# SwiGLU's gate and up products computed channel by token, with 512- and 256-column matmuls, in a fused two-block kernel

## The reference

```python
h = rmsnorm(x, ffn_norm_w[l])
x = x + (jax.nn.silu(h @ w_gate[l]) * (h @ w_up[l])) @ w_down[l]
...
return rmsnorm(x, final_norm_w)
```

## Time and profile before

| what | value |
|---|---|
| median of three runs | 2379.36 us (2378.09 to 2380.82) |
| the profiled execution, its own time | 2380.18 us |
| its span, first to last instruction | 2378.4 us |
| TensorE matmul (PE) | 2362.0 us busy, 99%, 11452 instructions |
| TensorE weight load (PEld) | 1939.2 us, 82% |
| VectorE (DVE) | 1426.4 us, 60% |
| ScalarE (ACT) | 1183.9 us, 50% |
| GpSimd (POOL) | 241.7 us, 10% |

### The profile page before, as it was taken

One profiled execution on the slowest core, in us unless ns is written; L12 is line 12 of the kernel. 1 busy time (PEld: TensorE's weight loads), 2 busy tenths in 40 slices (PEclk: granted clock), 3 DMA queues, 4 the chain that ended last, 5 costly groups with the idle time before them and its releaser, 6 DMA issues.

```text
span 2378.4 us, 28485 instructions
## 1 busy us (share of the span) xinstructions
PE 2362.0 (99%) x11452; PEld 1939.2 (82%) x11452; DVE 1426.4 (60%) x1701; ACT 1183.9 (50%) x1695; POOL 241.7 (10%) x336
## 2 busy tenths in 40 slices
PE   9999999999999999999999999999999999999998
PEld 7887888888888888888887778788888888888887
DVE  6655665665566545665865565576554554557775
ACT  6544454454445444555655455465444444446554
POOL 0053004305300430000000010000000000000000
PEclk9999999999999999999999999999999999999999
DMA  6565457446545655666665454456555555655554
GB/s 211 195 173 164 142 178 190 157 154 183 167 137 182 174 169 169 222 206 194 211 216 190 142 179 149 152 179 227 186 188 195 189 184 194 193 181 193 195 194 142
DMA packets 241073, 430.79 MB, mean 181 GB/s; under 512 B 32212, under 2 KB 35933, under 8 KB 240942
## 3 DMA queue, kind: packets, MB, share of 16 engines
q1 hardware_dynamic: 227808, 413.38, 54.4%
q10 hardware_dynamic: 13134, 15.60, 2.2%
HBM read 423.66 MB, written 5.29 MB: 180 GB/s over the span
## 4 chain that ended last, share of the span: by engine, by line
PE 89%; POOL 5%; DVE 2%; DMA 1%; issue 1%; ACT 1%; ACTq 0%; SPq 0%; POOLq 0%; DVEq 0%
PE gemm L1328 27%; PE gemm L1330 27%; PE gemm L1329 27%; POOL arena L2283 5%; PE side L904 3%; DMA arena<-delta_blocks 1%; DVE arena L1751 1%; DVE weight_lo L1745 1%; PE side L1251 1%; PE side L998 0%; PE side L1266 0%; PE side L1290 0%; DMA arena<-in_x_dram 0%; PE side L1064 0%; PE side L1220 0%
## 5 line engine op out<-in xcount | busy, mean ns | idle before, releaser
L1745 DVE TENSOR_TENSOR weight_lo<-weight_raw,weight_hi 128x1024 fp32r<-128x1024 f32 x780 | 970.5, 1248 | 736.3 <-ACT weight_hi L1356 735.0
L1356 ACT ACTIVATE weight_hi<-weight_raw 128x1024 fp32r<-128x1024 f32 x780 | 821.9, 1056 | 863.2 <-PE gemm L1330 822.7
L1328 PE MATMUL gemm<-weight_hi,x_hi 128*128 128x512 f32 x2368 | 943.8, 399 | 1.1 <-DVE weight_lo L1745 1.1
L1330 PE MATMUL gemm<-weight_hi,x_lo 128*128 128x512 f32 x2368 | 924.6, 390 | 0.0
L1329 PE MATMUL gemm<-weight_lo,x_hi 128*128 128x512 f32 x2368 | 924.0, 390 | 0.0
L1328 PEld LDWEIGHTS gemm<-weight_hi,x_hi 128*128 128x128 f32 x2368 | 445.4, 188 | 100.2 <-issue 9.7
L1330 PEld LDWEIGHTS gemm<-weight_hi,x_lo 128*128 128x128 f32 x2368 | 445.2, 188 | 94.3
L1329 PEld LDWEIGHTS gemm<-weight_lo,x_hi 128*128 128x128 f32 x2368 | 445.9, 188 | 88.9 <-issue 1.4
L1328 PE MATMUL gemm<-weight_hi,lhs_hi 128*128 128x512 f32 x736 | 287.4, 390 | 0.0
L1330 PE MATMUL gemm<-weight_hi,lhs_lo 128*128 128x512 f32 x736 | 286.8, 390 | 0.0
L1329 PE MATMUL gemm<-weight_lo,lhs_hi 128*128 128x512 f32 x736 | 286.7, 390 | 0.0
(11 more groups left out here) (186 smaller groups left out, 1024.0 us busy)
## 6 DMA issues: line engine op xcount, KB each, us to landing
weight_raw<-in_w_in_dram SPq DMA_DIRECT2D x207, 1024.0 KB, 5.1
weight_raw<-in_w_out_dram SPq DMA_DIRECT2D x48, 1024.0 KB, 5.1
weight_raw<-in_w_gate_dram SPq DMA_DIRECT2D x44, 1024.0 KB, 5.2
weight_raw<-in_w_up_dram SPq DMA_DIRECT2D x44, 1024.0 KB, 5.1
weight_raw<-in_w_down_dram SPq DMA_DIRECT2D x44, 1024.0 KB, 5.0
arena<-rel_line ACTq DMA_DIRECT2D x8, 384.0 KB, 5.3
arena<-delta_blocks ACTq DMA_DIRECT2D x16, 128.0 KB, 5.2
arena<-in_x_dram ACTq DMA_DIRECT2D x4, 512.0 KB, 6.0
```

Source lines behind the costliest of these rows:

```text
L1328: e.matmul(pair[i][:, :], xh[:, s], wh, start=first, stop=False)
L1330: m = e.matmul(pair[i][:, :], xl[:, s], wh, start=False, stop=last)
L1356: return e.activation(o, i, ACT.Copy, scale=scale)
L1745: return e.tensor_tensor(o, x, y, op)
```

## The change

For the gate and up jobs the roles of the operands are exchanged. The weights become the stationary operand, 128 channels at a time, and x the moving one. The high weights meet both parts of x in one matmul of 512 columns (256 of the high part, 256 of the low part, which now lie in one tensor), and the low weights meet the high part alone, in 256 columns. A job takes four PSUM banks, its own pair and two side banks, one for each 128 channels. Because the result now has channels on the partitions, `fturn` is gone, and the norm factor of a token is no longer a per-partition scalar: it is spread over all partitions once (`rdiag`, `rrow`) and multiplied in as a row. The two column halves of each bank are added at eviction (`fpart` on ScalarE, `both` on VectorE). Five steps of earlier stages are moved.

```diff
-            put(END[key] + 7, "dnorm", key, 0), put(END[key] + 7, "dnorm", key, 1)
+            put(END[key] + 8, "dnorm", key, 0), put(END[key] + 8, "dnorm", key, 1)
...
-            put(s + 8 + z, "dsc", g, q)
+            put(s + 8 + z // 2, "dsc", g, q)
...
-        s = END[f"mz{pr}"] + 2 if pr % 2 else END[f"dz{pr}"] + 45
+        s = END[f"mz{pr}"] + 3 if pr % 2 else END[f"dz{pr}"] + 45
...
+            put(s + 5, "rdiag", "r2"), put(s + 6, "rrow", "r2")
     for n in range(FFN // NC):
-        put(END[f"fg{n}"], "tanh", f"fg{n}"), put(END[f"fg{n}"] + 1, "silu", f"fg{n}")
-        s = END[f"fu{n}"]
-        put(s, "fact", n), put(s + 1, "fturn", n, 0), put(s + 1, "fturn", n, 2)
+        put(END[f"fg{n}"], "fpart", f"fg{n}"), put(END[f"fg{n}"], "fgate", n)
+        put(END[f"fg{n}"] + 1, "tanh", f"fg{n}"), put(END[f"fg{n}"] + 2, "silu", f"fg{n}")
+        put(END[f"fu{n}"], "fpart", f"fu{n}"), put(END[f"fu{n}"], "fact", n)
+        put(FIRST[f"fg{n}"], "across", f"fg{n}"), put(FIRST[f"fu{n}"], "across", f"fu{n}")
...
-    put(t + 1 + hp, "ggated", hp), put(t + 2 + hp, "gout", hp, 0), put(t + 2 + hp, "gout", hp, 2)
+    put(t + 1 + hp, "ggated", hp), put(t + 2 + 2 * hp, "gout", hp, 0), put(t + 2 + 2 * hp, "gout", hp, 2)
...
+                if kind_of(name) in ACROSS:
+                    for q, o in enumerate(across_banks(name)):
+                        s = slice(q * P, (q + 1) * P)
+                        e.matmul(o[:, :], wh[:, s], xboth[:, :, k0 + kk, :], start=first, stop=False)
+                        m = e.matmul(o[:, 0:T], wl[:, s], xh, start=False, stop=last)
+                    continue
...
+        def fpart(key):
+            low = claim("part", key)
+            w.wait_ge(*out_of(key))
+            for q, p in enumerate(across_banks(key)):
+                s = copy(low[:, q * T:(q + 1) * T], p[:, T:2 * T])
+            s.then_inc(sem("act:fpart"))
...
+        def both(o, name):
+
+            low = blk("part", name)
+            w.wait_ge(*at("act:fpart", name))
+            for q, p in enumerate(across_banks(name)):
+                s = tt(o[:, q * T:(q + 1) * T], p[:, 0:T], low[:, q * T:(q + 1) * T], ALU.add)
+            return s
+
+        def fgate(n):
+            z = claim("z", f"fg{n}")
+            w.wait_ge(*at("dve:rrow", "r2"))
+            w.wait_ge(*out_of(f"fg{n}"))
+            both(z, f"fg{n}").then_inc(sem("dve:fgate"))
+            w.wait_ge(*at("dve:fgate:sum", n))
+            tt(by_row(z, 4), by_row(z, 4), over(rrows[:, :], 1, 4), ALU.mult).then_inc(sem("dve:fgate"))
+
         def fact(n):
...
+            both(u, f"fu{n}").then_inc(sem("dve:fact"))
+            w.wait_ge(*at("dve:fact:u", n))
+            after(stt(z, z, 0.5, u, ALU.mult, ALU.mult))
+            tt(acts_all[:, 4 * n:4 * n + 4, :], by_row(z, 4), over(rrows[:, :], 1, 4), ALU.mult).then_inc(sem("dve:fact"))
```

More of the change, by code:

```diff
@@ L209, in evictions @@
         return [("act:tanh", name)]
+    if kind == "fg":
+        return [("dve:fgate:sum", number_of(name))]
     if kind in SILU:
@@ L373 @@
 STAGES = {
-    "norm": ("cols0", "cols", "xturn", "sqsum", "nscale"),
+    "norm": ("cols0", "cols", "xturn", "sqsum", "nscale", "rdiag", "rrow"),
     "kept": ("kept",), "gate": ("tanh", "silu", "mgate"),
@@ L384 @@
     "attn": ("alog", "aexp", "anorm", "aturn", "apv"),
-    "ffn": ("x2load", "res2", "fact", "fturn", "res4", "fweight", "tail"),
+    "ffn": ("x2load", "res2", "across", "fpart", "fgate", "fact", "res4", "fweight", "tail"),
 }
@@ L394 @@
             "dY": ("",), "donorm": ("mean", ""), "mscore": ("w", "den"), "msq": ("mean", ""),
-            "gsum": ("end", "rest", ""), "gstate": ("first", ""), "gsq": ("mean", ""), "alog": ("b", "")},
+            "gsum": ("end", "rest", ""), "fact": ("u", ""), "fgate": ("sum", ""), "gstate": ("first", ""), "gsq": ("mean", ""), "alog": ("b", "")},
     "pool": {"dinv": ("zero", "")},
@@ L398 @@
 for _engine, _names in {
-        "pe": "cols0 cols xturn gate1 fsum rel1 convturn dnorm dsc dT dX dv du0 dbu du1 do dout chan mdec mscore "
-              "mturn mnum mout ggate2 gsum gscore gkend gstate go gout alog aturn apv fturn",
+        "pe": "cols0 cols xturn rrow gate1 fsum rel1 convturn dnorm dsc dT dX dv du0 dbu du1 do dout chan mdec mscore "
+              "mturn mnum mout ggate2 gsum gscore gkend gstate go gout alog aturn apv",
         "act": "xturn sqsum kept tanh convtap convsilu dnorm dT du0 du1 donorm dout chan mexp mturn msq mout "
[L402 to L405, removed]
+               "ggabs ggexp ggln gkend gsq gout aexp aturn apv fpart",
+        "dve": "cols xturn rdiag rrow kept silu gate0 gate2 fsum rel0 rel1 convtap convsilu ddecay dsc dX dv dbu do "
+               "dgate mdec mm mden mgate mgated yb yhalf ya yres x1w gload ggate0 ggate2 ggate3 gscore ggated anorm res2 res4 "
+               "fweight",
         "pool": "nscale dss drhs dmask donorm dgate mrhs msq gsq anorm tail"}.items():
@@ L458, in block_table @@
             last = {"mo": ("dve:mgate", n), "dz": ("dve:dgate", n), "mz": ("dve:mgated", n), "gb": ("dve:yhalf", n),
-                    "ga": ("dve:yres", n), "gr": ("dve:ggated", n), "fg": ("pe:fturn", n, 2)}[kind]
-            live(("z", key), ("tanh", key), last)
+                    "ga": ("dve:yres", n), "gr": ("dve:ggated", n), "fg": ("dve:fact", n)}[kind]
+            live(("z", key), ("fgate", n) if kind == "fg" else ("tanh", key), last)
     live(("nar", "gates"), ("gate0",), ("pe:gate1",))
@@ L513, in block_table @@
             live(("ET", half, c), ("aturn", half, c), ("pe:apv", half, c))
+    for n in range(FFN // NC):
+        for key in (f"fg{n}", f"fu{n}"):
+            live(("part", key), ("fpart", key), ("dve:fgate:sum" if key[1] == "g" else "dve:fact:u", n))
+        live(("th", f"fg{n}"), ("tanh", f"fg{n}"), ("dve:fact", n))
+    live(("diag", "r2"), ("rdiag", "r2"), ("pe:rrow", "r2"))
     for z in range(3):
-        live(("tail", z), ("fturn", 8, 0), home=z)
+        live(("tail", z), ("fact", 8), home=z)
     return t
@@ L529, in bank_table @@
             t.append((step, step, ((f"{same[name]}:{name}",) + args,), None))
+        elif name == "across":
+            key = args[0]
+            done = ("dve:fgate:sum" if kind_of(key) == "fg" else "dve:fact:u", number_of(key))
+            for z in range(2):
+                t.append((step + (z,), step, (done,), 2 * ((JNUM[key] + 1) % 2) + z))
         elif name == "gate1":
@@ L1292, in apv, with across, rrow @@
             m.then_inc(sem("pe:apv"))
-        def fturn(n, c):
-            w.wait_ge(*at("dve:fact", n))
-            p = open_bank("fturn", n, c)
-            turn_pair(p, blk("z", f"fg{n}"), c).then_inc(sem("pe:fturn"))
+        def across(key):
+            for z in range(2):
+                open_bank("across", key, z)
+        def rrow(tag):
+            w.wait_ge(*at("dve:rdiag", tag))
+            p, d = open_bank("rrow", tag), blk("diag", tag)
+            for i in range(NT):
+                m = e.matmul(p[:, i * P:(i + 1) * P], ONE, d[:, i * P:(i + 1) * P], start=True, stop=True)
+            m.then_inc(sem("pe:rrow"))
         def product(idx, tiles=tuple(range(NT))):
@@ L2267, in vector_program @@
                      gscore=gscore, gstate=gstate, gsq=gsq, ggated=ggated, alog=alog, anorm=anorm, res2=res2, res4=res4,
-                     fact=fact, fturn=fturn, fweight=fweight, tail=tail)
+                     rdiag=rdiag, rrow=rrow, fgate=fgate, fact=fact, fweight=fweight, tail=tail)
         for slot in range(-AHEAD, NH + 2):
```

81 lines of the change are left out of this document (39 added, 42 removed).

## The result

The changed kernel takes 2399.16 us, the median of four runs (2397.96 to 2399.78). The kernel before, run beside it, takes 2378.90. The ratio is 1.0083, with a 95% interval of 1.0066 to 1.0101: 0.8% slower, 20.3 us. The forecast was 10.6 us faster, with a range up to 2384, so the miss is 31 us. The profiled execution took 2399.06 us, with a span of 2397.3.

The account below looks back on a forecast made before the run. TensorE, its matmuls filling 99% of the span, was taken as the bound. Transposes -9.8, `rrow` +0.2, moved steps -3.2 and `d0` +2.2 gave -10.6 us: median 2368.8 us, range 2363 to 2384.

Parts of the forecast that it names:

- The moved steps: `dnorm`, `mnum` to `mout` and `gout`, one slot later: four late-transpose waits on TensorE vanish, -3.2 us, with 0 as other end.
- Rival 4: Moved steps fail their purpose: the wait moves along or `dsc` finds its banks taken; 2372 to 2375 us, chance 0.08.
- `dsc`: Score groups issued two to a slot: taken at 0; only the third pair could find the four side banks taken.
- The matmuls: Gate and up: a pair of 512 and 256 columns takes 0.340 us, loads hidden, no change per block, 0 us.
- rivals 1 and 2: First: alternating widths keep gate and up unsettled, +14.7 us, chance 0.21, sign 0.232 and over; second's sign: 0.12 to 0.19.
- Rival 2: Gate and up: full loads show behind 256 columns, up to 0.077 us each, 2477 us; 7.5 ns a pair cancels gain; chance 0.06.
- The transposes: `fturn`'s 8 transposes per hidden group go: 0.89 us a group, 9.8 us saved over 11 groups.
- `d0`: Third slot of the first down job: TensorE waits once for the left rows' low part, +2.2 us, bounds 1.9 and 2.8.
- `rrow`: Two small matmuls added on TensorE to spread the norm factor, +0.2 us.
- rival 3: VectorE's chain misses the low weights at each `fact`: 0.5 us late, 11 times, is 5.5 us, 2374.3; chance 0.08.

Follow-up runs that it names:

- taking `tin` out of the way: Changed kernel with `tin` of the odd groups issued one slot later, so `msq` is ahead of it on ScalarE again: 2380.01 us, ratio 1.0004.
- half loads: Kernel with `tin` a slot later, loading 64 of 128 columns in most blocks of gate and up: high weights 2372.05 us, low weights (control) 2380.95 us.
- four and four: Kernel with `tin` a slot later, each gate and up block ordered as four 512-column matmuls, then four of 256: 2386.39 us, ratio 1.0035.
- `mnum` back: Changed kernel with `mnum`, `msq`, `mgated` and `mout` of the odd pairs put back one slot earlier: 2381.87 us, ratio 1.0011.
- `dsc` paired: Changed kernel with the other moved steps (`dnorm`, `mnum` to `mout`, `gout`) put back, `dsc` still issued two groups to a slot: 2385.07 us, ratio 1.0024.

## Why the prediction was wrong

**The moved steps (-3.2 taken, +18.5 measured, with `dsc`'s share in it).** This is the step that failed. "Each wait is shorter than the slot that it is given" compared the late transposes with the time given to them. It did not go through each engine's program in the slots to which the steps move. `msq`'s part on ScalarE moved behind `tin`. Undoing the one step gave 17.3 us, doing it alone cost 18.4, and taking `tin` out of the way gave 19.2. Rival 4 was that the moved steps do not pay, at up to 2375, 6.2 us above the forecast: the right place, but the term is off by 22, and the rival had no mechanism. The rest of the term held. `dnorm` at 508 gave 1.0 (0.93 forecast), `gout` 0.7 (0.68), and the first `dnorm`, which the prediction did not count, 0.5. For `mout` the waits in the earlier trace rows were read as waits for VectorE, which they are by their releaser; the chain behind was GpSimd, with `dinv` ahead of the power (in the kernel before `dinv` ends at 437.76, and the power runs right behind it, until 438.63). Whether a later slot would have helped there without the pairing and with `msq` ahead of `tin` was not run.

**`dsc` (0 taken, +5.3 measured).** The prediction looked at the side banks, and they are not the cost. What the pairing moves is TensorE's work ahead of the slot that issues `nin`, and from there `dinv` and the power. In the changed kernel itself this probably hides in part in the wait for `tin`; no run separates the two there.

**The matmuls (0 taken, +9.4 measured).** The two instances on which 0.340 rested were read as a load that fits into 0.1137 us with 3 ns of room. In a steady stream it does not fit: 0.117 behind a 256-column matmul, and 0.230 behind the next. Both lie just below the signs named for rivals 1 and 2 (0.232, 0.12), so the profile after alone could not tell the two apart; the half loads did. Rival 2 had the mechanism, at a chance of 0.06, the lowest of the four. Its threshold, 7.5 ns a pair for the whole gain, lies just above the 6.7 measured. How the cost is spread over the matmuls stays open, as the run with four and four shows. By the Trainium skill's "TensorE: Matmul & The Clock Gate" (part 2, "LDWEIGHTS (loading the stationary operand)") a load takes P/1.2 ns, 107 ns for 128 columns, which would fit under the 113.7 of the earlier trace rows; the runs with half loads show that it does not quite. Part 3's rule, that loads overlap only between different row groups, is again not borne out: by it whole loads would stand in each pair, not 6.7 ns.

**The transposes (-9.8).** Right: some -0.91 for a group, -10.0 for the eleven. Ten lie in the gate and up jobs, where the loads' +9.4 cancel them, the eleventh in the second slot of `d0`.

**`d0` (+2.2) and `rrow` (+0.2).** The wait at `d0` is 1.72 us and costs 2.0 with the slower steps behind it, between the bounds that the prediction gave. `rrow` costs 0.46: it was counted as 2 small matmuls, and the trace has 4.

**VectorE's chain at each `fact` (rival 3).** It did not show: there is no wait for `weight_lo` in the jobs after.

**What was not foreseen.** -1.7 us from two waits for `weight_lo` that are gone, since block N lives longer and another step gets a block that is free earlier. The full diff has that line; the prediction passed over it. The kernel before with that line and `gout`'s move shows the same -1.7.

**The sum.** Two `mout` +20.7, loads +9.4, `d0` +2.0, `rrow` +0.5, the start +0.6; transposes -10.0, `dnorm` -1.0 and -0.5, `gout` -0.7, N -1.7: +19.3, against +19.0 in the last row of the table. The +20.7 can't be split cleanly between `tin` and `dsc`, since both end in the same wait: the first alone gives 18.4 in the kernel before, and with `mnum` back 4.2 are left for the second.

## What to carry to other kernels

Before a step is moved in a table of slots, write out for each engine that takes part what stands ahead of it in the new slot; a DMA issue that waits for its source holds up all that is behind it on an in-order engine, and moving a step by one slot can put it on the other side of such a wait. A load of 128 columns under a 256-column float32r matmul cost 6.7 ns here, so a rearrangement that trades columns one for one but halves some of the matmuls has to be priced with that before its gain is counted. Where a term rests on some ns of room times a thousand, one instance in the trace is no bound.

## What the runs showed of the hardware

- With a full load under the 256 float32r columns the steady pair takes 0.3467 us, with a 64-column load there 0.340; behind each other such 256-column matmuls are 0.117 to 0.120 apart, though two full loads had been seen to start 0.11 apart. With four matmuls of 512 columns behind four of 256, those of 512 are 0.233 to 0.235 apart, against 0.2268 in the kernel before.
- The clock after a wait does not go by the wait's length alone. With `dsc` paired, 2.35 us of waiting at 441.35 were followed by a granted clock of 0.50, the 1.2 GHz level, for the transposes and some matmuls (0.42 us a step). With `mnum` back in the changed kernel, 3.14 us at 443.12 were followed by none of that: eight transposes in 1.09 us and a granted clock of 1.00, as these rows of its timeline and its windows show. At the other `mout` the two kernels wait equally long, 2.35 us at 863.41 and at 862.57, and again only the paired one has slow matmuls behind it (0.43 us a step, against 0.23). What makes the difference was not tried.

```profile
443.12 1.09 PE L922 MATMUL side<-constants,arena 128*128 128x128 f32 x8 [3.14 <-DVE arena L1783]
...
443.00:445.00 2.00, 1.88 (x13) 1.71 (x14) 0.07 (x1) 0.10 (x1) 0.00 (x0) 1.00 0.92 260
```
